# MLP of a two-layer trunk: one fused loop over 256 units, or the whole first product and then the whole second, through memory

## The chip, the cores and the metric

One core of one Trainium2 chip runs the whole kernel. The metric is the device time of one execution in microseconds (us); less is better. The profile is one execution's record of every instruction on the engines: TensorE (PE, with its weight loads as PEld), VectorE (DVE), ScalarE (ACT), GpSimd (POOL) and SyncE (SP), which only issues DMAs.

## The reference

Two layers over x of 1024 tokens x 1024 channels, float32. Each has a mixer (an mLSTM and a windowed attention behind one input projection, then an output projection), and behind it the part that is changed:

```python
h2 = _rmsnorm(x, norm2_g[l])                                   # 1024 x 1024
x = x + jnp.square(jax.nn.relu(h2 @ w_ff1[l])) @ w_ff2[l]      # 1024 x 4096, 4096 x 1024
```

## The kernel before

A float32 product is made of three float32r products: each operand is split into a high part (a cast by ScalarE) and a low part (the operand minus its high part, by GpSimd for weights, by VectorE for activations), and TensorE adds high x high, high x low and low x high in PSUM.

A layer has four stages with a barrier of all engines behind each: input projection, attention and convolution, mLSTM with output projection and residual, and the MLP. Each engine's order of work is written out by hand; semaphores that only count up order the engines against each other. Nothing is planned by a program.

The MLP goes over `CH = 16` chunks of 256 hidden units. For a chunk, `hidden_part` makes W1's product in the plain way: 2 x 128 units, 2 halves of 512 tokens, 8 blocks of 128 channels, 3 parts, so 96 matmuls of 512 columns into PSUM banks 6 and 7. ScalarE takes relu and square (`hidden`). The second product, `product`, is by Winograd's form of Strassen's scheme: the 256 units and 1024 columns of W2 and the 512 tokens of a half are cut into 2 x 2 blocks, and 7 block products stand in for 8. It wants sums of blocks: `u_sums` of the activations and `w2_sums` of W2, on VectorE. `u_his`, `w2_hi` and `w1_hi` on ScalarE cast, `u_los` on VectorE and `w1_lo`, `w2_lo` on GpSimd subtract. A chunk has 2 x 7 products of 6 matmuls, 84, and VectorE's `add` adds each of the 14 from two PSUM banks to x in SBUF (`xs`). Some products are accumulated in PSUM on one that has been added once already, so `product` waits for an earlier `add`.

TensorE's order (`halves`) puts 6 to 10 matmuls of the next chunk's first product behind each of the 14 block products, so a chunk of the loop is 84 + 96 = 180 matmuls, and 12 matmuls lie between one block product and the next. The first chunk's hidden product (`hidden_quarter`, 192 matmuls of 256 columns) lies in the norm at the MLP's start; the last chunk has no next one to be mixed with. VectorE's order is 14 adds with `u_sums`, `u_los` and `w2_sums` between them. SP loads W1 and W2 of a chunk (512 KB a DMA) when GpSimd is through with the one before.

## Time and profile before

| | us |
|---|---|
| median of 3 runs (lowest, highest) | 2406.27 (2405.28, 2407.17) |
| profiled execution, whole | 2407.71 |
| its span, first to last instruction | 2405.9 |
| TensorE busy | 2279.0 |
| VectorE busy | 1536.9 |
| ScalarE busy | 801.7 |
| GpSimd busy | 827.4 |
| mean granted TensorE clock, as a share of full speed | 0.969 |

"Busy" counts every instruction from start to end; matmuls overlap, so the step from one start to the next is what a matmul costs. Layer 0's MLP lies at 501 to 1206 us of the span, layer 1's at 1700 to 2406. In a profile's line, L1592 is the line of the code, then come engine, operation, output <- inputs, shape and count.

### The profile page before, as it was taken

To read this page: it belongs to the slowest core of one execution; us is meant where nothing else is said; L and a number is where in the kernel's file an instruction comes from. 1 tells how busy PE (TensorE), PEld (TensorE's weight loads), DVE (VectorE), ACT (ScalarE), POOL (GpSimd) and SP (SyncE) were. 2 spreads that over 40 slices of the span, in tenths; PEclk is the share of its full clock that TensorE was granted. 3 is DMA by queue.
4 is the path that set the end of the run, shared out by engine and by line. 5 is a ranking of instruction groups with operands and counts; after the bars stand their busy time and mean duration, and the time that the engine had idled before them with its cause. 6 is when DMAs were issued, how large, how long until landed. Compare 5 with 4: busy or idle time off the path is not lost.

```text
span 2405.9 us, 36025 instructions
## 1 busy us (share of the span) xinstructions
PE 2279.0 (95%) x12356; PEld 1923.3 (80%) x12356; DVE 1536.9 (64%) x1838; ACT 801.7 (33%) x1436; POOL 827.4 (34%) x641
## 2 busy tenths in 40 slices
PE   6999979988999999999879999799799999999997
PEld 6988868877888888888679888688778888888886
DVE  4048753356777778777740487533567777777876
ACT  4133332233333333333241334322333333333331
POOL 4235421233242424334142453221333424242431
PEclk9999989989999999999989999899899999999999
DMA  6222332202011121211142222322011211112111
GB/s 252 94 70 72 104 110 66 96 18 70 35 52 52 35 70 35 70 35 52 45 150 84 66 86 90 109 66 96 26 63 35 70 35 54 51 35 70 35 52 70
DMA packets 83368, 166.87 MB, mean 69 GB/s; under 512 B 18008, under 2 KB 45272, under 8 KB 83168
## 3 DMA queue, kind: packets, MB, share of 16 engines
q1 hardware_dynamic: 68064, 142.79, 18.0%
q10 hardware_dynamic: 15232, 23.16, 2.7%
q8 instruction: 40, 0.66, 0.1%
q14 instruction: 32, 0.26, 0.0%
HBM read 138.57 MB, written 31.54 MB: 71 GB/s over the span
## 4 chain that ended last, share of the span: by engine, by line
PE 84%; DVE 6%; issue 6%; ACT 2%; POOL 1%; ACTq 1%; DVEq 0%; SPq 0%; POOLq 0%
PE ps L958 29%; PE ps L1229 24%; PE ps L1212 23%; DVE xs L1592 2%; DVE ul L1617 2%; PE ps L1054 1%; PE ps L1130 1%; PE ps L1124 1%; PE ps L1153 1%; PE ps L949 1%; PE ps L1154 1%; DVE y L1278 1%; PE ps L1082 1%; PE ps L1069 1%; PE ps L1126 1%
## 5 line engine op out<-in xcount | busy, mean ns | idle before, releaser
L1592 DVE TENSOR_TENSOR xs<-ps,xs 128x1024 f32<-128x1024 f32 x448 | 546.9, 1221 | 310.1 <-PE ps L1229 307.5
L1229 PE MATMUL ps<-w2h,uh 128*128 128x512 f32 x896 | 356.0, 397 | 35.2 <-DVE xs L1592 19.4
L1212 PE MATMUL ps<-hTh,w1h 128*128 128x512 f32 x960 | 374.2, 390 | 0.0
L1212 PE MATMUL ps<-hTl,w1h 128*128 128x512 f32 x960 | 374.1, 390 | 0.0
L1212 PE MATMUL ps<-hTh,w1l 128*128 128x512 f32 x960 | 374.1, 390 | 0.0
L912 POOL TENSOR_TENSOR w2l<-raw,w2h 128x512 fp32r<-128x512 f32 x128 | 169.1, 1332 | 586.8 <-ACT w2h L700 586.8
L1229 PE MATMUL ps<-w2l,uh 128*128 128x512 f32 x896 | 351.2, 392 | 0.0
L1229 PE MATMUL ps<-w2h,ul 128*128 128x512 f32 x896 | 350.8, 392 | 0.0
L1229 PEld LDWEIGHTS ps<-w2h,uh 128*128 128x128 f32 x896 | 169.3, 189 | 86.6 <-DVE xs L1592 36.3
L912 POOL TENSOR_TENSOR w2l<-tS,w2h 128x512 fp32r<-128x512 f32 x96 | 172.8, 1802 | 183.3 <-ACT w2h L700 183.3
L1212 PEld LDWEIGHTS ps<-hTl,w1h 128*128 128x128 f32 x960 | 180.7, 188 | 38.0
L1212 PEld LDWEIGHTS ps<-hTh,w1h 128*128 128x128 f32 x960 | 180.8, 188 | 37.7
L1212 PEld LDWEIGHTS ps<-hTh,w1l 128*128 128x128 f32 x960 | 180.5, 188 | 37.8
L1229 PEld LDWEIGHTS ps<-w2h,ul 128*128 128x128 f32 x896 | 169.5, 189 | 36.1
L1229 PEld LDWEIGHTS ps<-w2l,uh 128*128 128x128 f32 x896 | 169.7, 189 | 33.8
L908 POOL TENSOR_TENSOR w1l<-rawf,w1h 128x1024 fp32r<-128x1024 f32 x64 | 155.8, 2437 | 99.4 <-ACT w1h L691 95.9
L958 PE MATMUL ps<-whi,hTh 128*128 128x258 f32 x640 | 184.3, 288 | 1.9 <-POOL wlo L834 0.9
L707 ACT ACTIVATE uq<-ps 128x512 f32<-128x512 f32 x120 | 71.8, 599 | 338.4 <-PE ps L1212 335.0
L958 PE MATMUL ps<-wlo,hTh 128*128 128x258 f32 x640 | 181.9, 284 | 0.0
L958 PE MATMUL ps<-whi,hTl 128*128 128x258 f32 x640 | 181.5, 284 | 0.0
L722 ACT CAST uh<-uq 128x1024 fp32r<-128x1024 f32 x64 | 67.3, 1052 | 291.1 <-DVE uS L1609 291.1
L958 PE MATMUL ps<-hTh,whi 128*128 128x512 f32 x384 | 156.0, 406 | 0.0
(198 smaller groups left out, 4295.9 us busy)
## 6 DMA issues: line engine op xcount, KB each, us to landing
raw<-in_wstream SPq DMA_DIRECT2D x104, 512.0 KB, 4.5
rawf<-in_wstream SPq DMA_DIRECT2D x64, 512.0 KB, 4.6
raw<-in_wtoken SPq DMA_DIRECT2D x20, 516.0 KB, 6.1
zD<-zst ACTq DMA_DIRECT2D x80, 129.0 KB, 1.8
xt<-out_y SPq DMA_DIRECT2D x16, 512.0 KB, 3.4
out_y<-xs SPq DMA_DIRECT2D x16, 512.0 KB, 4.0
zq<-zD SPq DMA_DIRECT2D x16, 320.0 KB, 2.7
xs<-in_x ACTq DMA_DIRECT2D x8, 512.0 KB, 11.1
```

The costliest lines, as they stand in the source:

```text
L707: nc.scalar.activation(uq[b][:, a, :], ps[:, bank, :], ACT.Relu).then_inc(f_rel, 1)
L722: nc.scalar.copy(uh[b][:, 0:4, :], uq[b][:].rearrange("p a (h c) -> p (a h) c", c=256)).then_inc(u_hi, 1)
L908: nc.gpsimd.tensor_tensor(w1l[:, a, :], raw1[a][:], w1h[:, a, :].bitcast(F32), ALU.subtract).then_inc(m1_lo, 1)
L912: nc.gpsimd.tensor_tensor(w2l[:, r, :], w2_from(r), w2h[:, r, :].bitcast(F32), ALU.subtract).then_inc(m2_lo, 1)
L949: mm = pe.transpose(ps[:, bank + k // 4, (k % 4) * P:(k % 4) * P + P], ybuf[t % 2][:, k * P:(k + 1) * P], ident[:])
L958: mm = pe.matmul(out_ap, a, b, start=(c == 0), stop=(c == n - 1))
L1054: pe.matmul(ps[0:64, SB + h // 4, m * P:(m + 1) * P], qS[b0:b0 + DH, m * P:m * P + 64], kw0[b0:b0 + DH, :], start=True, stop=True)
L1069: mm = pe.transpose(ps[:, TB + h // 4, (h % 4) * P:(h % 4) * P + P], pr[:, h, :], ident[:])
L1212: mm = pe.matmul(ps[:, 6 + a, :], w, x, start=(c % 24 == 0), stop=(c % 24 == 23))
L1229: mm = pe.matmul(ps[:, BANK[r] + tp, :], u, w[:, r, :], start=(r < 3 and j == 0), stop=(j == 2), skip_group_check=True)
L1592: V.tensor_tensor(y, ps[:, BANK[r]:BANK[r] + 2, :], y, ALU.add).then_inc(f_acc, 1)
L1617: V.tensor_tensor(ul[b][:, 4:7, :], uS[:], uh[b][:, 4:7, :].bitcast(F32), ALU.subtract).then_inc(u_lo, 1)
```

## The change

The MLP is cut in two phases.

**Phase 1** makes the whole of W1's product. Chunks 0 and 1 (`STD = 2`) are made in the plain way (192 matmuls of 256 columns, 96 of 512). Chunks 2 to 15, called steps here, (`pair_1`) are by seven block products too: 128 units x 512 channels x 512 tokens each, 12 matmuls, 84 a step. For this three block sums of the normed activations are made once a layer (`t_step`, ten VectorE ops of 2048 elements; `sum_hi` on ScalarE, `sum_lo` on GpSimd) and `w1_sums` for each step (4 VectorE ops of 512). The seven products are put together into four blocks by ScalarE's `first_copy` and five VectorE adds of a PSUM bank and an SBUF row (`f_w`). Then come relu and square, `u_sums`, `u_his` and `u_los` as before, each now over all 1024 tokens, and `store_u` on SP writes high and low parts of the seven blocks to a DRAM tensor `uD`: eight DMAs a step, 1 KB runs. SBUF for this is won by spilling x (`xs`) to `out` and reading it back.

**Phase 2** makes the second product over `GR = 8` groups of 512 units. `product_2` has 12 matmuls (two units of 256 accumulate in PSUM), 168 a group; `load_u` reads a group's u, 8 DMAs. `add` is needed once for 12 matmuls instead of once for 6. `w2_sums`, `w2_hi` and `w2_lo` work on 1024 elements at once instead of 512, once a group.

Semaphores of small ops in other stages are merged, and `hTh`, `hTl` become one tensor `hT` in another order, with the same instructions.

The pieces of the diff below belong, in their order, to SP (`store_u` to `stream_2`), ScalarE (the first `phase_1`), GpSimd (`sum_lo`, `w1_lo`), TensorE (`pair_1`, `product_2`) and VectorE (the second `phase_1` and all behind it).

```diff
-        hTh = wide("hTh", [P, KT, S], F32R)
-        hTl = wide("hTl", [P, KT, S], F32R)
+        hT = wide("hT", [P, 2, 2, KT, 512], F32R)
...
+        uD = nc.dram_tensor("uD", [CH, 2, P, 7, 2, 256], F32, kind="Internal").ap()
...
+        ORD1, ORDZ = (1, 6, 5, 2, 7, 3, 4), (2, 1, 6, 5, 7, 3, 4)
+        ORD2 = (1, 5, 6, 3, 7, 2, 4)
+        PARTS = ((4, 7), (0, 4))
...
+                def store_u(j, c):
+
+                    for part in range(2):
+                        i0, i1 = PARTS[part]
+                        sp.wait_ge(u_hi, l * (2 * CH) + (j * 4 + (2 * c + part + 1)))
+                        alone(sp)
+                        for b in range(2):
+                            sp.dma_start(uD[j * 2 + c, b, :, i0:i1, 0, :], uh[:, i0:i1, b * 256:b * 256 + 256].bitcast(F32)).then_inc(u_hst, 16)
...
+                def stream_1(j, c):
+
+                    sp.wait_ge(m1_lo, l * FM + (j * 14 + (7 * (c - STD) + 4 * STD + 7)))
+                    alone(sp)
+                    if c == 0:
+                        load_w1(j, 1, raw1)
+                        store_u(j - 1, 1)
+                    else:
+                        load_w1(j + 1, 0, raw1)
+                        store_u(j, 0)
...
+                def stream_2(g, first):
+
+                    sp.wait_ge(m2_lo, l * (7 * GR) + (g * 7 + 7))
+                    alone(sp)
+                    load_w2(g + 1)
...
+                    for b in range(2):
+                        load_u(g + 1, b, 0, g * 14 + (7 * b + 4))
+                        load_u(g + 1, b, 1, g * 14 + (7 * b + 7))
...
+                def phase_1(j, c):
...
+                        hidden(jp, cp, 3, A12, None, f_w, added(l, jp, cp, 5))
+                    w1_hi(j, c, 6)
+                    first_copy(j, c, made(l, j, c, 1))
+                    u_his(jp, cp)
+                    w1_hi(jn, cn, 0); w1_hi(jn, cn, 1); w1_hi(jn, cn, 2)
+                    hidden(j, c, 0, A11, ps[:, 4 * s, :], f_m, made(l, j, c, 2))
+                    w1_hi(jn, cn, 3)
+                    hidden(j, c, 1, A22, None, f_w, added(l, j, c, 3))
+                    w1_hi(jn, cn, 4)
+                    hidden(j, c, 2, A21, None, f_w, added(l, j, c, 4))
+                    w1_hi(jn, cn, 5)
...
+                sum_lo(0, 1); sum_lo(1, 2)
+                w1_lo(1, 0, 0); w1_lo(1, 0, 1); w1_lo(1, 0, 2)
+                sum_lo(2, 4)
+                sum_lo(3, 3)
+                for pos in range(3, 7):
+                    w1_lo(1, 0, pos)
...
+                def pair_1(j, c):
+
+                    o = 4 * (c % 2)
+                    pe.wait_ge(f_rel, l * (4 * CH) + (j * 8 + 4 * (c - 1)))
+                    for pos, (r, bank, first) in enumerate(((1, 0, True), (6, 1, True), (5, 2, True), (2, 0, False), (7, 3, True), (3, 2, False), (4, 3, False))):
+                        pe.wait_ge(m1_lo, made(l, j, c, r))
+                        if r in (2, 3, 4):
+                            pe.wait_ge(f_w, added(l, j, c, {2: 1, 3: 2, 4: 3}[r]))
...
+                        product_1(r, o + bank, first, True)
...
+                def product_2(g, b, r, first):
...
+                    if r in (6, 7, 3, 4):
+                        pe.wait_ge(y_acc, n + POS2[{6: 1, 7: 6, 3: 5, 4: 7}[r]] + 1)
...
+                def phase_1(j, c):
...
+                        V.tensor_tensor(up, ps[:, (4 - o) + 3, :], up, ALU.add).then_inc(f_w, 1)
+                    u_sums(jp, cp)
+                    dve.wait_ge(f_m, made(l, j, c, 6))
+                    dve.wait_ge(f_m1, l * (CH - STD) + (j * 2 + (c - 1)))
+                    V.tensor_tensor(u[:, A12, :], ps[:, o + 1, :], u[:, A12, :], ALU.add).then_inc(f_w, 1)
+                    u_los(jp, cp, 0)
+                    dve.wait_ge(f_m, made(l, j, c, 5))
+                    dve.wait_ge(f_w, added(l, j, c, 1))
+                    V.tensor_tensor(u[:, A22, :], ps[:, o + 2, :], u[:, A12, :], ALU.add).then_inc(f_w, 1)
+                    w1_sums(jn, cn)
+                    u_los(jp, cp, 1)
+                    dve.wait_ge(f_m, made(l, j, c, 7))
+                    dve.wait_ge(f_w, added(l, j, c, 2))
+                    V.tensor_tensor(u[:, A22, :], ps[:, o + 3, :], u[:, A22, :], ALU.add).then_inc(f_w, 1)
+                    dve.wait_ge(f_m, made(l, j, c, 3))
+                    V.tensor_tensor(u[:, A21, :], ps[:, o + 2, :], u[:, A12, :], ALU.add).then_inc(f_w, 1)
...
+                u_los(LAST, 0, 1)
+                dve.wait_ge(f_m, FZ + POSZ[7] + 1)
+                dve.wait_ge(f_w, AZ + 3)
+                V.tensor_tensor(u[:, A22, :], ps[:, 7, :], u[:, A22, :], ALU.add).then_inc(f_w, 1)
...
+                w2_sums(0, 1)
+                u_sums(LAST, 1)
+                add(0, 0, 1, True)
+                u_los(LAST, 1, 0)
+                add(0, 0, 5, True)
+                u_los(LAST, 1, 1)
...
+                def half_1(g, first, more):
+                    add(g, 1, 1, first)
                     if more:
-                        w2_sums(p + 1, 0)
-                    add(p, 1, 0)
+                        w2_sums(g + 1, 0)
+                    add(g, 1, 5, first)
+                    if more:
+                        w2_sums(g + 1, 1)
+                    for r in (6, 3, 7, 2, 4):
+                        add(g, 1, r, first)
```

## Rows read from the trace of the kernel before

**Rows 1.** The page, part 1: busy time, share and instructions of each engine.
```profile
PE 2279.0 (95%) x12356; PEld 1923.3 (80%) x12356; DVE 1536.9 (64%) x1838; ACT 801.7 (33%) x1436; POOL 827.4 (34%) x641
```

**Rows 2.** Stretches of layer 0's MLP: length, busy us of each engine, clock, DMA.
```profile
549.00:1172.50 623.50, 618.15 (x2700) 506.95 (x2700) 476.96 (x450) 215.15 (x312) 228.18 (x135) 1.00 0.14 47
1172.50:1200.00 27.50, 22.57 (x85) 16.23 (x84) 19.42 (x20) 3.01 (x4) 0.44 (x1) 0.94 0.20 77
```

**Rows 3.** Chain of waits inside the loop: start us, us, what.
```profile
788.45 1.36 PE ps L1212 x6
...
792.35 1.63 DVE ul L1617
```

**Rows 4.** Timeline of VectorE and GpSimd in the loop: start us, us, what.
```profile
761.07 2.53 DVE L1603 TENSOR_TENSOR uS<-uq 128x256 f32<-128x256 f32 x1
...
771.95 0.95 DVE L1617 TENSOR_TENSOR ul<-uS,uh 128x768 fp32r<-128x768 f32 x1
...
792.35 3.01 DVE L1617 TENSOR_TENSOR ul<-uS,uh 128x768 fp32r<-128x768 f32 x1
795.28 1.21 DVE L1592 TENSOR_TENSOR xs<-ps,xs 128x1024 f32<-128x1024 f32 x1
...
802.55 2.53 DVE L1603 TENSOR_TENSOR uS<-uq 128x256 f32<-128x256 f32 x1
...
792.13 2.40 POOL L908 TENSOR_TENSOR w1l<-rawf,w1h 128x1024 fp32r<-128x1024 f32 x1
794.50 2.00 POOL L912 TENSOR_TENSOR w2l<-tS,w2h 128x512 fp32r<-128x512 f32 x1
...
798.98 1.29 POOL L912 TENSOR_TENSOR w2l<-tS,w2h 128x512 fp32r<-128x512 f32 x1
```

**Rows 5.** The same two engines behind the norm of layer 0's MLP.
```profile
533.29 1.23 DVE L1284 TENSOR_TENSOR hTl<-ps,hTh 128x1024 fp32r<-128x1024 f32 x1 [2.24 <-ACT hTh L483]
...
537.95 1.51 DVE L1603 TENSOR_TENSOR uS<-uq 128x256 f32<-128x256 f32 x1
...
539.14 2.88 POOL L912 TENSOR_TENSOR w2l<-raw,w2h 128x512 fp32r<-128x512 f32 x2
```

**Rows 6.** Groups by line: busy us, mean ns of one, idle before.
```profile
L1592 DVE TENSOR_TENSOR xs<-ps,xs 128x1024 f32<-128x1024 f32 x448 | 546.9, 1221 | 310.1 <-PE ps L1229 307.5
...
L1614 DVE TENSOR_TENSOR ul<-uq,uh 128x1024 fp32r<-128x1024 f32 x64 | 77.8, 1216 | 2.2 <-ACT uh L722 2.2
...
L707 ACT ACTIVATE uq<-ps 128x512 f32<-128x512 f32 x120 | 71.8, 599 | 338.4 <-PE ps L1212 335.0
L722 ACT CAST uh<-uq 128x1024 fp32r<-128x1024 f32 x64 | 67.3, 1052 | 291.1 <-DVE uS L1609 291.1
```

**Rows 7.** DMA queues by packets, and a W2 load's issues and landing.
```profile
q1 hardware_dynamic: 68064, 142.79, 18.0%
q10 hardware_dynamic: 15232, 23.16, 2.7%
...
800.53 0.92 SPq L418 DMA_DIRECT2D raw<-in_wstream  x2
...
DMA to landing us min/median/max: 3.2/4.0/8.4
```

**Rows 8.** Timeline of TensorE around its waits in layer 0's MLP.
```profile
540.56 0.28 PE L958 MATMUL ps<-hTh,w1l 128*128 128x256 f32 x1
548.71 0.79 PE L1229 MATMUL ps<-w2h,uh 128*128 128x512 f32 x1 [7.87 <-ACT uq L714]
...
1184.52 0.74 PE L1229 MATMUL ps<-w2h,uh 128*128 128x512 f32 x1 [2.38 <-DVE xs L1592]
...
1188.04 0.40 PE L1229 MATMUL ps<-w2h,ul 128*128 128x512 f32 x1
...
1199.04 0.40 PE L1229 MATMUL ps<-w2h,ul 128*128 128x512 f32 x1
```

More of the change, by code:

```diff
@@ L392, in load_c @@
                     sp.dma_start(xt[p][:], out_t[i]).then_inc(c_xt[p], 16)
+                    if not (first or (isinstance(j, int) and i < 2)):
+                        sp.dma_start(out_t[i - 2], xs[:, i - 2, :]).then_inc(s_spill, 16)
                 def unit_c(k):
@@ new lines, in _, with load_w2, load_u @@
+                stream_1(1, 0); stream_1(1, 1)
+                with sp.Fori(2, LAST) as j:
+                    stream_1(j, 0); stream_1(j, 1)
+                stream_1(LAST, 0)
+                def load_w2(g):
+                    for k in range(2):
+                        for a in range(2):
+                            sp.dma_start(raw2[:, k, a, :], wstream[l, g * 8 + (UB + UC + 4 * k + 2 + a)]).then_inc(m2_raw, 16)
+                def load_u(g, b, part, upto):
+                    i0, i1 = ((0, 4), (4, 7))[part]
+                    if upto is not None:
+                        sp.wait_ge(y_m, l * YM + upto)
+                        alone(sp)
+                    for k in range(2):
+                        sp.dma_start(uk[b][k][:, i0:i1].bitcast(F32), uD[g * 2 + k, b, :, i0:i1]).then_inc(u_ld[b][part], 16)
@@ new lines, in _ @@
+                sp.wait_ge(f_m, l * FM + FM - 7 + POSZ[6] + 1)
+                alone(sp)
+                for t in (0, 1):
+                    sp.dma_start(xs[:, t, :], out_t[t]).then_inc(s_x[t], 16)
+                sp.wait_ge(f_m, l * FM + FM - 7 + POSZ[5] + 1)
+                alone(sp)
+                for t in (4, 5):
+                    sp.dma_start(xs[:, t, :], out_t[t]).then_inc(s_x[t], 16)
+                store_u(LAST, 0)
+                sp.wait_ge(f_m, l * FM + FM)
+                alone(sp)
@@ L931, in _ @@
+                with pool.Fori(2, LAST + 1) as j:
+                    for c in range(2):
+                        for pos in range(7):
+                            w1_lo(j, c, pos)
+                with pool.Fori(0, GR) as g:
+                    for r in ORD2:
+                        w2_lo(g, r)
                 barrier(pool, p_pool, (p_pe, p_sp, p_dve, p_act), l * PHASES + 4)
@@ new lines, in product_1 @@
+                def product_1(r, bank, first, last):
+                    xh, xl = right(r)
+                    s = SLOT[r]
+                    for k in range(4):
+                        h_, l_ = w1s[:, s, 0, k * P:k * P + P], w1s[:, s, 1, k * P:k * P + P]
+                        for i, (w, x) in enumerate(((h_, xh), (h_, xl), (l_, xh))):
+                            mm = pe.matmul(ps[:, bank, :], w, x[:, k, :], start=(first and k == 0 and i == 0), stop=(k == 3 and i == 2),
+                                           skip_group_check=True)
+                    mm.then_inc(f_m, 1)
@@ L1248, in _ @@
+                for b in range(2):
+                    for r in ORD2:
+                        product_2(0, b, r, True)
+                alone(pe)
+                with pe.Fori(1, GR) as g:
+                    for b in range(2):
+                        for r in ORD2:
+                            product_2(g, b, r, False)
                 barrier(pe, p_pe, (p_act, p_sp, p_dve, p_pool), l * PHASES + 4)
@@ new lines, in raw_of, with t_step @@
+                def raw_of(t):
+                    return tf[t][:, 1]
+                def t_step(n, out_, a, b, op):
+                    if n in (2, 3, 4, 5, 6, 9):
+                        dve.wait_ge(t_sum, l * 10 + n)
+                    V.tensor_tensor(out_, a, b, op).then_inc(t_sum, 1)
+                H = {k: v.bitcast(F32) for k, v in b_at_h.items()}
+                L = {k: v.bitcast(F32) for k, v in b_at_l.items()}
+                Z = [hTf[:, 1, i, 0:4, :] for i in range(2)]
+                SUB = ALU.subtract
@@ new lines, in _, with w2_sums @@
+                phase_1(1, 0); phase_1(1, 1)
+                with dve.Fori(2, LAST) as j:
+                    phase_1(j, 0); phase_1(j, 1)
+                phase_1(LAST, 0)
+                def w2_sums(g, part):
+                    n = l * (4 * GR) + g * 4
+                    b11, b12, b21, b22 = [raw2[:, :, a, c:c + 512] for a in range(2) for c in (0, 512)]
+                    if part == 0:
+                        dve.wait_ge(m2_raw, l * (64 * GR) + (g * 64 + 64))
+                        V.tensor_tensor(tS[0][:], b12, b11, ALU.subtract).then_inc(m2_sum, 1)
```

733 lines of the change are left out of this document (434 added, 299 removed).

## The prediction

> **What bounds the kernel now.** I read the page first: TensorE is busy 95% of the span, VectorE 64%, GpSimd 34% [rows 1]. The reader is to see from this that only work on TensorE, or something that makes TensorE wait, can move the time. The table of stretches of layer 0 then shows where TensorE isn't fed [rows 2]: the MLP's loop, 549.0 to 1172.5, holds 2700 matmuls in 623.5 us, and the last chunk's 84 matmuls take 27 us. One matmul of 512 columns starts 1.36 / 6 = 0.227 us after the one before [rows 3]. So 180 of them, one chunk of the loop, need 40.8 us; the first op of its `u_sums` comes back after 802.55 - 761.07 = 41.5 us [rows 4]. The 0.7 us between is the key to this change, and the chain of waits shows where it comes from [rows 3]: a subtraction on VectorE (`u_los`) ends the row of matmuls. The subtraction of 768 elements at 792.35 took 3.01 us, while another instance of the same line took 0.95 [rows 4]. GpSimd held its own subtraction from 792.13 to 794.53, and VectorE finished 0.83 us after that; the GpSimd op behind it took 2.00 instead of 1.29 us [rows 4]. At 539 both engines had work waiting, and they took turns: three 256-element ops of VectorE took 1.5 us each, the first at 537.95, while GpSimd's of 512 took 1.44 [rows 5]. The adds that read PSUM were never held up: the mean of 448 is 1221 ns, and one ran its usual 1.21 us at 795.28 inside a GpSimd op [rows 4, 6]. I call this **the turn**: a VectorE op with both inputs in SBUF and a GpSimd op do not overlap; the one that comes first runs to its end.
>
> **Prices.** VectorE with two SBUF inputs: 1.22 us at 1024 elements and 0.95 at 768, so by the slope 0.68 at 512 (0.6 from start to start), 1.75 at 1536 and 2.3 at 2048. GpSimd: 1.29 at 512, 2.4 at 1024, so 4.6 at 2048. ScalarE: 1.05 at 1024, 0.60 at 512, so 1.5 and 1.9 at the larger two. Add of 512 from PSUM: 0.68, as in SBUF, since the 1024 cost the same [rows 4, 6]. Two loads of 512 KB: 0.5 between the issues and 4.0 to land, so 4.5 us [rows 7].
>
> **What is removed.** Per layer the first product falls from 1536 matmuls of 512 columns (counting 192 of 256 columns as 96) to 192 in two plain chunks and 14 x 84 = 1176 in the others. That is 168 fewer, 38.1 us a layer, 76 us in all. The second product keeps its 1344. The Trainium skill's TensorE: Matmul & The Clock Gate, Back-to-back issue gap, gives N / 2.4 + 2.5 ns, 216 ns, where this trace has 227; by the page the gain would be 72.5 us. Layer 0 needs 658.9 us now, from the last small matmul's start at 540.56 to the last one's end at 1199.44 [rows 8]. After the change TensorE's own work there is (96 + 1176 + 1344) x 0.2267 = 593.1 us. The waits decide the rest.
>
> **First phase, one step of 84 matmuls, 19.05 us.** Seven products of 2.72 us. VectorE does five adds from PSUM (3.3 us), `u_sums` and `w1_sums` (8 x 0.6), `u_los` (1.75 + 2.3); GpSimd does seven `w1_lo` (9.0). The turn is thus held 8.9 + 9.0 = 17.9 of 19.05 us, and in a fixed order. I walk one step from its first matmul, with GpSimd three subtractions behind, as it turns out to be: four `w1_lo` alternate with the four `u_sums`, the last `w1_lo` ends at 5.4 and `u_sums` at 6.7; add for product 2, 7.4; `u_los` of 1536 can start at 7.7, when ScalarE's `u_his` has ended, and ends 9.4; add, 10.1. SP issues the next W1 at 5.5, and it lands at 10.0. `w1_sums` with one `w1_lo` between takes 3.8, to 13.9; `u_los` of 2048, 16.2; add, 16.9. Only then may product 4 start, due at 16.3. It ends at 19.7 to 20.0, with GpSimd again behind by three. Turned round once more it settles near **20.1 us, 1.05 over**. Bounds: 0 if turns fall well, 2.5 if one more GpSimd op gets in front of `u_los`. Twelve such steps: 12.6 us (0 to 30).
>
> **Start.** `t_step` adds ten VectorE ops of 2048 elements (23 us) and four GpSimd ops of 2048 (18.4), while the first `w1_lo` wait behind them in GpSimd's order. From the end of the norm at 534.5 [rows 5] to the add ahead of product 4 in `phase_1(1, 0)` the turn must be held 23 + 18.4 + 8.1 (`u_los` twice) + 4.9 (`u_sums` twice) + 4.9 (`w1_sums` twice) + 10.3 (eight `w1_lo`) = 69.6 us, to 604; the load of W1 for the step behind adds some 5 in which nobody can use it, and the add 0.7, so product 4 starts near 610 to 611. TensorE could be there at 540.6 + 21.8 + 16.3 = 578.7. That is 32 us of waiting in four or five pieces; now it is 7.9 [rows 8]. After a stall of 2.38 us TensorE ran 8 matmuls at 0.427 us each, a half-speed stretch that cost 1.6 us [rows 8]; most of these stretches lie ahead of another wait, I add 2. Together 34 (20 to 45).
>
> **Between the phases.** In the last step `w2_sums` and the first two `w2_lo` (2.4 each) stand on VectorE and the turn ahead of `u_los`, which stands ahead of the add that product 4 needs: 22.8 instead of 16.3, 6.5 late. Then `add(0, 0, 1)`, needed by the third product of phase 2, stands behind `w2_sums(0, 1)` and `u_sums(LAST, 1)`, which waits for ScalarE's last squares, and ScalarE waits in order for the third `w2` sum; four `w2_lo` of 2.4 us get turns between the four sums. I get 11 us, and 2 more for the next two adds. With a slow stretch 22 us (6, if no turn falls badly, to 30).
>
> **Second phase, a group of 168 matmuls, 38.1 us.** Half 0 has only adds: no wait. In half 1 (time from its first matmul) the first add ends 4.1, as GpSimd starts `w2_lo` to 6.4. Two 1024-element `w2_sums` end at 8.8, the add of product 5 at 10.0: product 3, due 8.2, waits 1.8. The next `w2_lo` holds 8.9 to 11.3, the other two sums end 13.6, the add of product 6 at 14.9, and product 7, due 12.7, waits 2.2. **4.0 us a group, seven groups: 28 a layer.** Bounds: with no turn lost, 0.3 a group; with the half-speed stretch after each, 6. I add 3 for a few stretches: mine are a little shorter than the 2.38 us that had one. So 31 (2 to 42). The end of the layer, now 27.5 us for 84 matmuls [rows 2], needs no wait any more; that is in the 593.1.
>
> **The stores and loads through memory.** A step stores 3.67 MB in 3584 runs of 1 KB, 224 for each of 16 DMA engines. The ACT queue q10 carried 15232 packets of 1.5 KB on average in 2.7% of 16 engines' span, 68 ns each [rows 7]; at that price, too high for 1 KB, the stores take 15.3 us. W1's 16 packets of 4 KB for each engine take 3.2 at q1's 102 ns for 2.1 KB. That is 18.5 of 20 us. SP needs 0.5 us for each of ten issues. Its `store_u` stands behind the wait for the last `w1_lo`, at 5.5, when the first half of `u_his` is ready only at 7.5, so it is late for nothing; the last store is issued at 16.4, lands some 4 us later, and `first_copy`, which waits for it, is due at 22.9. In phase 2 a group loads 7.3 MB of u and 2 of W2 in 38 us, issued most of a group ahead. So 0, with the bound in the rivals. The spill of x before phase 3 and its return lie beside the norm and the last W1 step. Other edits (merged semaphores, the order inside `hT`) cost nothing: the same instructions on the same queues.
>
> **Sum.** 593.1 + 34 + 12.6 + 22 + 31 = 692.7 against 658.9: 34 us more a layer, 68 in all. Against the profiled execution, 2407.7 with a span of 2405.9, and so 1.4 above the median shown, this gives 2475 us.
>
> **Rivals.** (1) *The turn costs little*: ops queue so that VectorE mostly comes first, waits at the lower bounds: 20 + 0 + 6 + 2 = 28 a layer, so 593.1 + 28 = 621, 38 less: 2330. Halfway, 2400. For it: VectorE has 36% idle, and the loop now loses only 0.7 us to it. Against: at 539 the two alternated strictly. It decides once the waits in a layer sum to less than 66 us. (2) *Memory binds the first phase*: each step becomes its eight stores and two loads. If the stores went one by one, each at half the 4.0 us that a load takes to land [rows 7], a step would need 8 x 2.0 + 4.5 = 20.5 to 22 us, 28 steps x 1.9 = 50 more at the upper end: 2525. Against: loads issued 0.5 us apart land together. The Trainium skill's DMA: Bandwidth & Descriptors, Anatomy of one DMA, gives 2.0 us plus bytes / 436 GB/s for each; eight in a row would be 24 us and two loads 6, an estimate of 2700 for the kernel, if nothing overlapped. (3) *Half speed after every stall*: 1.6 us behind each of 14 groups and half of the steps, 45 more: 2520. (4) *It does what it says and only that*: 76 less and the old edges stay, 2330, the same time as (1) and as unlikely.
>
> **Chances.** Forecast (2420 to 2510) 0.63; (1) with (4) 0.18, of which 0.15 faster and 0.03 within 0.2% (what a measurement of this kernel can tell from none); (2) 0.07; (3) 0.12. Slower 0.82. The range 2398 to 2530 leaves out most of (1) and the worst of (2).
>
> **What would show it.** TensorE's starts of one first-phase step 20 us apart, with a gap ahead of its last product released by VectorE; in phase 2 two gaps of 1.8 and 2.2 us in every second half; `w2_sums` at 2 us and more where alone they'd take 1.2; 30 us of gaps behind 562. I am wrong if `u_los` and the sums run at their bare prices, or if gaps are released by a DMA.

## The result, and the profile after

The changed kernel takes 2469.07 us, the median of 4 runs (2465.62 to 2472.09), beside 2405.99 us (2405.28 to 2407.17, 4 runs) of the kernel before: ratio 1.0261, 95% interval 1.0243 to 1.0279. It is 63 us slower; 68 were forecast. Its profiled execution took 2465.62 us.

The page after, parts 1 and 3: busy time, share and instructions of each engine, and the DMA queues.
```profile
PE 2231.7 (91%) x12020; PEld 1875.0 (76%) x12020; DVE 1470.6 (60%) x1632; ACT 858.2 (35%) x1444; POOL 1065.7 (43%) x685
...
q1 hardware_dynamic: 209888, 394.47, 45.9%
```
TensorE has the 336 fewer matmuls that were promised, 12020 instead of 12356 [rows 1], and the span is longer all the same: it is waits that were bought. VectorE has less to do than before, GpSimd more, and q1 moves 394 MB instead of 143 [rows 7].

Timeline of TensorE in layer 0 of the kernel after: start us, length, what, and in brackets the idle time before it and what ended it. The end of a group is modelled, so the time lost at a wait is start minus start, less 0.2267 us for each matmul between.
```profile
537.28 2.98 PE L1183 MATMUL ps<-hT,w1s 128*128 128x256 f32 x17
...
591.14 11.19 PE L1445 MATMUL ps<-hT,w1s 128*128 128x512 f32 x36 [12.93 <-DVE uf L1920]
606.86 4.61 PE L1445 MATMUL ps<-tT,w1s 128*128 128x512 f32 x12 [4.53 <-DVE uf L1929]
...
843.60 3.03 PE L1445 MATMUL ps<-tT,w1s 128*128 128x512 f32 x12 [1.31 <-DVE uf L1929]
867.53 5.49 PE L1445 MATMUL ps<-tT,w1s 128*128 128x512 f32 x12 [4.24 <-DVE uf L1982]
888.52 24.60 PE L1493 MATMUL ps<-w2s,uk 128*128 128x512 f32 x96 [9.74 <-DVE xs L1961]
921.33 4.59 PE L1493 MATMUL ps<-w2s,uk 128*128 128x512 f32 x12 [8.21 <-DVE xs L1961]
927.95 37.27 PE L1493 MATMUL ps<-w2s,uk 128*128 128x512 f32 x156 [2.03 <-DVE xs L1961]
966.71 3.01 PE L1493 MATMUL ps<-w2s,uk 128*128 128x512 f32 x12 [1.49 <-DVE xs L1961]
971.27 35.66 PE L1493 MATMUL ps<-w2s,uk 128*128 128x512 f32 x156 [1.55 <-DVE xs L1961]
1008.41 3.02 PE L1493 MATMUL ps<-w2s,uk 128*128 128x512 f32 x12 [1.49 <-DVE xs L1961]
...
1225.07 1.29 PE L1493 MATMUL ps<-w2s,uk 128*128 128x512 f32 x5
```
The last small matmul starts near 539.2 and the last one of the layer near 1226.1: 687 us, where 692.7 were forecast and 658.9 were needed before [rows 8]. TensorE's own work was taken at 593.1, so 94 us are lost, and the rows say where. The last product of the first pair starts at 606.86 and could have at 539.2 + 168 x 0.2267 = 577.3: 29.6. From there twelve steps take 843.60 - 606.86 = 236.7, or 19.73 each, 0.68 over the 19.05 of their matmuls: 8.2. The last step gives 23.93, 4.9 late, and the 36 matmuls from 867.53 to 888.52 take 20.99 instead of 8.16, 12.8 late. In group 0 the 96 matmuls from 888.52 and the 12 from 921.33 lose 11.0 and 3.9. Then each of six groups has two waits: 971.27 - 966.71 - 2.72 = 1.84 and 1008.41 - 971.27 - 35.37 = 1.77, 3.61 a group and 21.7 in six; 1.6 more is a slow stretch behind 927.95.

VectorE in the second phase of the kernel after, groups by line and shape, 941 to 1199 us: busy us, mean ns.
```profile
L1944 DVE TENSOR_TENSOR raw<-raw 128x1024 f32<-128x1024 f32 x6 | 20.5, 3424 | 0.0
L1947 DVE TENSOR_TENSOR tS<-raw,tS 128x1024 f32<-128x1024 f32 x6 | 13.5, 2251 | 0.0
```
Four subtractions of one size: the first and the last (L1943 and L1949, not shown, 1216 and 1226 ns) run at their bare 1.22 us, and two take 3.42 and 2.25. These are the two waits of a group, nearly as the walk had them: the second sum stands behind the first `w2_lo` (the walk had the first sum behind it too), the third behind the rest of the second.

VectorE and SyncE in the first group of the second phase: the wait that nobody had forecast.
```profile
917.78 1.23 DVE L1943 TENSOR_TENSOR tS<-raw 128x1024 f32<-128x1024 f32 x1 [8.83 <-DMA raw<-in_wstream]
...
888.39 9.62 SPq L476 DMA_DIRECT2D uD<-uh  x4
...
904.81 4.28 SPq L508 DMA_DIRECT2D raw<-in_wstream  x4
```
VectorE waits for the W2 of group 1, which SyncE issues only at 904.8, behind the eight stores of the last chunk's u, the first of them at 888.4. It is used 13.0 us after its issue, where a load of W2 before took 4.0 to land [rows 7]. The last `w2_lo` of group 0, for which the load waits, had ended at 889.6.

Stretches of the kernel after: the steps of the first phase, the turn between the phases, the second phase.
```profile
606.86:843.60 236.74, 233.69 (x1009) 189.44 (x1009) 189.82 (x181) 150.00 (x217) 145.81 (x85) 0.99 0.70 240
843.60:927.95 84.35, 60.13 (x228) 47.50 (x228) 54.61 (x38) 28.07 (x33) 37.82 (x16) 0.86 0.89 332
927.95:1226.30 298.35, 280.12 (x1212) 227.66 (x1212) 169.84 (x125) 46.80 (x45) 122.84 (x47) 0.99 0.57 209
```
The last two numbers are the busy share of the 16 DMA engines and GB/s. It was 0.14 in the loop before [rows 2]; now it is 0.70 in the first phase and 0.89 between the phases.

### The profile page after: what moved, and what is told of

Read it like the earlier page. It is cut to its first block, busy times and chain, and to the rows that moved or that the text cites. A ratio compares the mean times of both kernels' runs of the same rounds, so it can differ in the third digit from the quotient of the medians.

```text
span 2463.8 us, 36690 instructions
## 1 busy us (share of the span) xinstructions
PE 2231.7 (91%) x12020; PEld 1875.0 (76%) x12020; DVE 1470.6 (60%) x1632; ACT 858.2 (35%) x1444; POOL 1065.7 (43%) x685
## 4 chain that ended last, share of the span: by engine, by line
PE 57%; issue 20%; POOL 9%; DVE 6%; SPq 4%; DMA 2%; ACT 1%; ACTq 0%; POOLq 0%; DVEq 0%
PE ps L1183 28%; PE ps L1493 19%; POOL w1s L1124 8%; SPq L476 2%; DVE xs L1961 2%; DVE tS L1947 1%; PE ps L1445 1%; POOL tT L1131 1%; PE ps L1278 1%; SPq L482 1%; PE ps L1174 1%; PE ps L1354 1%; PE ps L1348 1%; DMA raw<-in_wstream 1%; PE ps L1377 1%
## 5 line engine op out<-in xcount | busy, mean ns | idle before, releaser
L1493 PE MATMUL ps<-w2s,uk 128*128 128x512 f32 x2688 | 628.5, 395 | 76.9 <-DVE xs L1961 76.9
L1493 PEld LDWEIGHTS ps<-w2s,uk 128*128 128x128 f32 x2688 | 509.6, 191 | 195.7 <-DVE xs L1961 89.8
L1961 DVE TENSOR_TENSOR xs<-ps,xs 128x1024 f32<-128x1024 f32 x224 | 273.9, 1223 | 268.8 <-PE ps L1493 267.3
L1445 PE MATMUL ps<-hT,w1s 128*128 128x512 f32 x1344 | 322.9, 397 | 37.2 <-DVE uf L1920 25.9
L1445 PEld LDWEIGHTS ps<-hT,w1s 128*128 128x128 f32 x1344 | 258.2, 193 | 93.8 <-DVE uf L1920 26.7
L1445 PE MATMUL ps<-tT,w1s 128*128 128x512 f32 x1008 | 251.6, 404 | 29.2 <-DVE uf L1929 17.8
L1445 PEld LDWEIGHTS ps<-tT,w1s 128*128 128x128 f32 x1008 | 193.3, 194 | 82.9 <-DVE uf L1929 30.0
L1183 PE MATMUL ps<-hT,whi 128*128 128x512 f32 x768 | 245.7, 401 | 0.0
L1183 PE MATMUL ps<-whi,hT 128*128 128x258 f32 x1280 | 239.0, 286 | 2.0 <-DVE hT L1539 1.4
L1183 PEld LDWEIGHTS ps<-whi,hT 128*128 128x128 f32 x1280 | 201.6, 191 | 4.0 <-issue 3.5
```

The costliest lines, as they stand in the source:

```text
L1183: mm = pe.matmul(out_ap, a, b, start=(c == 0), stop=(c == n - 1))
L1445: mm = pe.matmul(ps[:, bank, :], w, x[:, k, :], start=(first and k == 0 and i == 0), stop=(k == 3 and i == 2), skip_group_check=True)
L1493: mm = pe.matmul(ps[:, bank + tp, :], u, w2s[r][:, w, k, :], start=(r in (1, 2, 5) and k == 0 and i == 0), stop=(k == 1 and i == 2), skip_ ...
L1961: V.tensor_tensor(y, ps[:, bank:bank + 2, :], y, ALU.add).then_inc(y_acc, 1)
```

## The experiments

My theory was the turn: a VectorE op with two inputs in SBUF and a GpSimd op exclude each other, and with that the order of the queues sets the waits. The rivals were the plain length of VectorE's queue, and memory. Unless it is said otherwise, a kernel is the changed one with one edit. The kernel before ran beside each on its chip, at 2405.2 to 2405.8 us. One thing must be kept in mind: the twelve steps of the first phase are not equally long from trace to trace. In layer 0 they take 236.7 us in the changed kernel's trace and 239.8 to 244.6 in those of the next three edits and of the order between the phases, none of which touches that phase. Differences of a few us between two kernels can come from there.

**The sums of W2 in half 0.**
```
 with dve.Fori(1, GR - 1) as g:
     for r in ORD2:
         add(g, 0, r, False)
+        if r in (3, 7, 2, 4): w2_sum(g + 1, {3: 0, 7: 1, 2: 2, 4: 3}[r])
-    half_1(g, False, True)
+    half_1(g, False, False)
```


> Groups 1 to 6 of the second phase make the next group's four w2_sums one by one behind the last four adds of half 0, where GpSimd has nothing to do, instead of in half 1. My theory (the turn): a sum takes its bare 1.22 us there and fits the 1.5 us that VectorE has between two adds, each w2_lo takes its bare 2.4 us, and the two waits of TensorE in every half 1 (1.84 and 1.77 us, 3.61 a group) go: 12 x 3.61 = 43 us less, 2426 us. Rival one (memory): the next W2 has not landed by then, VectorE waits for it with the adds of half 0 behind, and TensorE waits in half 0 instead: 2460 to 2480 us. Rival two (the waits come from the PSUM banks or the loads of u, not from the sums): no change, 2469.


Measured 2426.30 us (2421.38 to 2430.54, 4 runs), 42.8 less than 2469.07, ratio to before 1.0089 (1.0066 to 1.0111). TensorE then runs the rest of the layer in one piece. Timeline of TensorE, and groups of VectorE and GpSimd from 945 to 1199 us:
```profile
931.00 275.32 PE L1493 MATMUL ps<-w2s,uk 128*128 128x512 f32 x1212 [1.49 <-DVE xs L1973]
...
L1961 DVE TENSOR_TENSOR raw<-raw 128x1024 f32<-128x1024 f32 x6 | 7.3, 1214 | 0.0
L1135 POOL TENSOR_TENSOR w2s<-raw,w2s 128x1024 fp32r<-128x1024 f32 x24 | 57.6, 2399 | 122.2 <-ACT w2s L944 122.2
```
The op that took 3424 ns takes 1214 where GpSimd is idle. All 1212 matmuls follow one another. The time is the forecast to the microsecond, with some luck: in layer 0 the stretch of six groups lost its waits and its slow stretch, 23 us where the forecast counted 21.7, while the twelve steps took 4.9 us longer in this trace.

**GpSimd's op in the second phase cut short.** It leaves out 448 of 512 columns of `w2_lo`, where ScalarE puts a copy of W2's tile; the sums stay in half 1.
```
 w2_hi: + nc.scalar.copy(w2s[r][:, 1, :, 64:512], w2_from(r)[:, :, 64:512])
 w2_lo: nc.gpsimd.tensor_tensor(w2s[r][:, 1, :, 0:64], w2_from(r)[:, :, 0:64], ..., ALU.subtract)
```


> In the second phase GpSimd's w2_lo subtracts 64 of each 512 columns only (128 elements, some 0.5 us instead of 2.4); ScalarE copies the other 448 columns of W2's tile there, which is not the remainder that the computation wants. The sums stay where the changed kernel has them, in half 1. It tells the turn from the plain length of VectorE's queue. The turn: two sums of 1.22, the first late by one short op, end before the add of product 5 is due to matter; the waits of 1.84 and 1.77 us in half 1 fall under 0.3 each, the sums run at 1.2 to 1.7 us, and between the phases 13 us of held time go too: 2405 to 2425 us. Rival (the sums delay the adds by their own length): both waits stay within 0.3 us of what they are, 2465 us.


One run, 2433.27 us. Timeline of TensorE, and one of each op from VectorE's and GpSimd's:
```profile
925.62 43.77 PE L1494 MATMUL ps<-w2s,uk 128*128 128x512 f32 x180 [14.29 <-DVE xs L1962]
969.95 38.37 PE L1494 MATMUL ps<-w2s,uk 128*128 128x512 f32 x168 [0.56 <-DVE xs L1962]
1008.89 1.43 PE L1494 MATMUL ps<-w2s,uk 128*128 128x512 f32 x5 [0.57 <-DVE xs L1962]
```
```profile
963.54 1.48 DVE L1945 TENSOR_TENSOR raw<-raw 128x1024 f32<-128x1024 f32 x1
...
963.24 0.70 POOL L1136 TENSOR_TENSOR w2s<-raw,w2s 128x128 fp32r<-128x128 f32 x1 [21.30 <-ACT w2s L945]
```
A group now takes 1008.89 - 969.95 = 38.94 us, 0.86 over its matmuls instead of 3.61, with the four sums in the same places. So at least three quarters of the wait came from GpSimd's op. The rest isn't all queue: the second and third sum, 1.48 and 1.42 us, are still 0.26 and 0.2 late beside the short op. The total missed its 2405 to 2425: the wait for group 1's W2 grew to 14.3 us, since TensorE reached it sooner and the load, counted from the end of the twelve steps, came only 1 us sooner; those steps took 5.2 us longer in this trace.

**Group 1's W2 issued ahead of the last stores.**
```
-store_u(LAST, 1)
 def stream_2(g, first):
     sp.wait_ge(m2_lo, l * (7 * GR) + (g * 7 + 7))
     load_w2(g + 1)
     if first:
+        store_u(LAST, 1)
```


> Only SyncE's order between the phases is changed: the load of group 1's W2 is issued ahead of the stores of the last chunk's u instead of behind them. In the changed kernel that load is issued at 904.8, when the stores at 888.4 to 904.5 are out, and VectorE waits 8.8 us for it, which TensorE sees as 8.2 and 2.0 us of waiting in group 0 and a slow stretch behind. My theory: the load goes out as soon as the last w2_lo of group 0 is done (889.6) and lands before half 1; group 0 then has the two waits of 1.8 us that the other groups have. 10.2 + 0.6 - 3.6 = 7 us and 1.6 of slow clock, 9 us a layer, 18 in all: 2451 us. Rival (the load waits for the bandwidth that the stores and u's loads take, not for its place in the queue): it lands late all the same, 2465 to 2470.


Measured 2453.54 us (2445.88 to 2458.57), 15.5 less, for 18 forecast. Timeline of TensorE:
```profile
898.02 24.68 PE L1493 MATMUL ps<-w2s,uk 128*128 128x512 f32 x96 [9.65 <-DVE xs L1961]
924.18 3.04 PE L1493 MATMUL ps<-w2s,uk 128*128 128x512 f32 x12 [1.48 <-DVE xs L1961]
928.74 35.68 PE L1493 MATMUL ps<-w2s,uk 128*128 128x512 f32 x156 [1.53 <-DVE xs L1961]
```
Group 0 has the two waits of every other group. The long one came from the load's place in SyncE's order.

**The four large subtractions of the start on VectorE.**
```
 def sum_lo(n, t): ...
-    nc.gpsimd.tensor_tensor(lo_, raw_, hi.bitcast(F32), ALU.subtract)
+    V.tensor_tensor(lo_, raw_, hi.bitcast(F32), ALU.subtract)
```
with its four calls moved from GpSimd's order into VectorE's, behind u_sums(0, 0), t_step 5, w1_sums(1, 0) and u_sums(0, 1).

> At the start of the first phase the four subtractions of 2048 elements that GpSimd makes (sum_lo) are put on VectorE, where one takes 2.3 us instead of 4.5; nothing else. My theory (the turn: what counts is the sum of what both engines hold): 4 x (4.5 - 2.3) = 9 us less of held time ahead of product 4 of the first pair, which starts near 598 instead of 606.9; 9 us a layer, and with a slow stretch less 18 to 22 in all: 2449 us. Rival one (VectorE's own queue is the bound, GpSimd's work is beside it): 9.2 us more on VectorE, 2 x 9 more, 2487. Rival two (the start waits for the load of W1 in the first step, 6.5 us in the trace, whatever comes before): no change, 2469.


Measured 2445.23 us (2443.37 to 2447.28), 23.8 less, ratio 1.0162 (1.0145 to 1.0179). To give VectorE, the busier of the two, nine microseconds more work a layer made the kernel faster, as it should if GpSimd's eighteen are gone from the same turn; that VectorE's queue alone is the bound, which forecast 2487, is refuted. Timeline of TensorE:
```profile
599.49 2.88 PE L1435 MATMUL ps<-tT,w1s 128*128 128x512 f32 x12
```
Product 4 starts at 599.5 instead of 606.9; 598 was forecast. That is 7.4 us, and in layer 1, counted from the same matmuls, it is 9.6: 17 of the 23.8. The rest lies in the steps behind and isn't explained by the edit: in layer 0 of this trace W1 was used 4.9 to 7.0 us after its issue, and product 4 of the twelfth step starts at 843.42, not sooner than in the changed kernel.

**The order between the phases.**
```
-w2_sums(0, 0)
 u_los(LAST, 0, 1)
 ... add of product 7 ...
+w2_sums(0, 0)
 ...
-u_sums(LAST, 1); add(0, 0, 1); u_los(LAST, 1, 0); add(0, 0, 5); u_los(LAST, 1, 1); adds 6, 3, 7, 2, 4
+adds 1, 5, 6; u_sums(LAST, 1); add(0, 0, 3); u_los(LAST, 1, 0); adds 7, 2; u_los(LAST, 1, 1); add(0, 0, 4)
```


> VectorE's order between the phases: w2_sums(0, 0) behind u_los(LAST, 0, 1) and the add of product 7, on which product 4 waits; and the first three adds of phase 2 ahead of u_sums(LAST, 1), whose results only the stores of the last chunk's u need, with u_sums and u_los in the gaps of half 0. Nothing is left out. My theory: TensorE's waits of 4.2 and 9.7 us there come from this order and the turn. The first falls under 1 us; the second to about 2 us (the third sum stands behind add 4, then comes w2_lo of product 6). 4 + 7 = 11 us less a layer, with a slow stretch less 12 to 14; against it the last stores and so group 1's W2, which stands behind them, come 4 to 8 us later and lengthen the wait of 8.2 us by as much. Net 2 x 6 = 12 less: 2457 us, and the wait in half 1 of group 0 over 10 us. Rival (the held time itself is the bound, order does not matter): within 3 us of 2469.


Measured 2469.50 us (2466.64 to 2473.87): nothing, where 12 less were forecast. The wait of 4.2 us went, that of 9.7 fell to three of 1.8, 3.7 and 1.1, 8 us in all for 11 forecast, and all of it came back in one place, the wait for group 1's W2, 18.3 instead of 8.2. Timeline of TensorE:
```profile
877.29 11.22 PE L1493 MATMUL ps<-w2s,uk 128*128 128x512 f32 x48 [1.76 <-DVE xs L1961]
892.24 9.79 PE L1493 MATMUL ps<-w2s,uk 128*128 128x512 f32 x36 [3.73 <-DVE xs L1961]
...
924.46 5.20 PE L1493 MATMUL ps<-w2s,uk 128*128 128x512 f32 x12 [18.29 <-DVE xs L1961]
```
I had written this down as the price against, 4 to 8 us of 12; it was all that was won.

**Each store of u made twice** (the second to a memory of its own).


> Each store of u is made twice, the second to a memory of its own that nobody reads; SyncE issues 18 DMAs a step instead of 10, and ScalarE's waits for the stores count both. In the changed kernel the DMA engines are busy 0.69 of a step of 19.4 us, 13.4 us, of which W1's load takes some 3.2. If that price holds, a step has 23.6 us of work for them: with 14 steps a layer at 4 to 5 us more, 115 to 140 us in all, 2585 to 2610 us, the DMAs having had a third of room. If the stores were hidden with much room (my prediction's term of nothing, at its 15.3 us a step for the stores), the same side. Rival (each DMA's fixed time, not its bytes, is what would bind, and eight were not far from it): 28 steps of 34 us or more, 2850 us. Rival two (the stores lie beside everything): 2469.


One run, 2664.51 us, above the 2585 to 2610 forecast and far below 2850. Stretch of nine steps of layer 0:
```profile
648.74:884.35 235.61, 194.48 (x756) 156.11 (x756) 135.75 (x135) 111.14 (x163) 106.47 (x63) 0.89 0.97 320
```
A step takes 235.61 / 9 = 26.2 us with the DMA engines busy 0.97 of it: 25.4 us of work for them, where the changed kernel has 0.70 x 19.73 = 13.8. The 3.67 MB of stores cost 11.6 us, not the 15.3 of my sum and not the 10.2 of this expectation. The time of the DMA engines binds here, and the rival with a fixed time for each DMA, 34 us or more a step, is out; whether it is bytes or the number of packets that costs, this run doesn't tell. My size was low: a step is 6.5 us longer, not 4 to 5, and the stretch between the phases grew as well: in group 0 TensorE waited 29.8 us for group 1's W2, where it had waited 8.2.

**All four edits together.**


> The four edits together: w2_sums in half 0, the W2 load of group 1 ahead of the last stores, sum_lo on VectorE, the new order between the phases. If they add up as timed alone against 2469 (43, 15.5, 24 and 0 less) the time is 2386 us, 0.8% under the kernel before. My theory says more than that: the new order alone brought TensorE 7 us ahead, all of which went into a longer wait for group 1's W2; with that load no longer behind the stores it should count, 5 to 7 us a layer: 2374 us. Rival (memory binds between the phases, where the DMA engines are busy 0.92 of the time): the loads of u, x and W2 only land later, 2386 to 2395 us, with TensorE's waits in group 0 released by DMAs or by adds that wait for x.


Measured 2394.23 us (2389.93 to 2397.04), ratio to before 0.9956 (0.9942 to 0.9969). It is the first version under the kernel before, but the 2374 of my theory fell; the rival's 2386 to 2395 stands. SyncE and VectorE between the phases:
```profile
877.96 2.97 SPq L508 DMA_DIRECT2D raw<-in_wstream  x4
...
897.96 1.23 DVE L1945 TENSOR_TENSOR tS<-raw 128x1024 f32<-128x1024 f32 x1 [9.11 <-DMA raw<-in_wstream]
```
W2 is now issued 27 us earlier and lands 17 to 20 us after its issue: the DMA engines are busy 0.96 from 840 to 870 and 0.89 from 870 to 925 us.

**The last stores later still**, on the kernel with the four edits.
```
 stream_2(0, True)
+store_u(LAST, 1)
-with sp.Fori(1, GR - 1) as g:
+with sp.Fori(1, GR - 2) as g:
     stream_2(g, False)
+stream_2(GR - 2, False, True)     # waits for the last chunk's stores
```


> The kernel with the four edits, and the stores of the last chunk's u moved once more, behind all loads of group 1 (only group 7 reads that chunk; its loads wait for the stores). In the kernel with four edits group 1's W2 is issued at 878.0 and lands 17 to 20 us later, with the stores issued right behind it and x and u loading before it; the DMA engines are 0.89 to 0.96 busy there. My theory now (memory binds between the phases, as bytes in flight together): without those 3.67 MB, 10 us at 366 GB/s, W2 lands near 888, TensorE's wait of 9.6 us in half 1 of group 0 falls to 1 or 2, and the 3.6 us in group 1, released by the W2 of group 2 that lands late, goes too: 10 us a layer, 2374 us. Rival (each transfer in its place of the queue, the stores behind take nothing from it): within 3 us of 2394.


Measured 2404.17 us (2396.76 to 2412.21, 12 runs), 10 us slower than with the four edits, where 20 faster were forecast. TensorE and SyncE:
```profile
944.80 252.61 PE L1484 MATMUL ps<-w2s,uk 128*128 128x512 f32 x1104 [8.66 <-DVE xs L1976]
```
```profile
920.90 2.99 SPq L476 DMA_DIRECT2D uD<-uh  x4
...
931.14 4.49 SPq L508 DMA_DIRECT2D raw<-in_wstream  x4
```
Group 1's W2 came hardly sooner: TensorE's wait for it is 8.2 us, not 9.6, so the stores behind it were not what mainly held it. What loads ahead of it (half of group 0's u and four tiles of x, 5.8 MB) is left as the likely cause. And the stores now stand ahead of group 2's W2, which made the wait in group 1 8.7 us instead of 3.6, some 5 us a layer. The first phase took 4.8 us longer in layer 0 of this trace than in that of the four edits, which the edit does not explain.

**Three more changes of order**, on the kernel just shown: u_sums(LAST, 1) one add later, the w2_sums of group 0 behind the adds of products 5 and 6, and at the start ScalarE's last plain square ahead of `sum_hi(3, 3)`.


> As the run above, and three changes of order: u_sums(LAST, 1) one add later; in half 1 of group 0 the two w2_sums behind the adds of products 5 and 6 instead of 1 and 5; at the start ScalarE's last plain square ahead of the third t copy, so that u_sums(0, 1) on VectorE, now idle for 4.2 us ahead of it, can start. Under the turn and the queues as read from the traces: 4 us a layer at the start (part of a wait of 12.8 us), 1 to 3 us a layer between the phases: 10 to 14 us under the run above, near 2362 us. Rival (the start is bound by the load of W1 behind it, or by held time alone, wherever the idle lies): no difference to the run above.


Measured 2403.49 us (2397.99 to 2411.85, 11 runs): no difference to the run above, so the rival stands. TensorE's start:
```profile
580.26 10.56 PE L1436 MATMUL ps<-hT,w1s 128*128 128x512 f32 x36 [6.36 <-POOL w1s L1125]
597.64 4.95 PE L1436 MATMUL ps<-tT,w1s 128*128 128x512 f32 x12 [6.81 <-DVE uf L1932]
```
The wait ahead of product 2 fell by half and came back ahead of product 4. How much of that is held time and how much is the load of W1 behind it, this run does not tell.

**W1's load alone on the queues**, on the kernel with the four edits, which ran again beside it as the measure.
```
 load_w1(j + 1, 0, raw1)
+sp.wait_ge(m1_raw[0], l * (16 * CH) + (j * 32 + 64))
 store_u(j, 0)
```
and the same in the other branch.

> The kernel with the four edits once more, as the measure for the next two on the same chip. Its first phase depends on when W1 lands: VectorE waited 7.8 us for it between 640 and 850 us of that kernel's trace and 12.5 us in that of the run with the later stores, though both have the same program there. If that is memory and not the program, this time falls between 2394 and 2404 us and its trace shows between 8 and 13 us of such waits.

> The four edits, and in the first phase SyncE waits until W1 has landed before it issues the stores of u that now follow 2 us behind the load. My theory: those stores are what lengthens the load's landing from 4.5 to 5 or 6 us; alone it lands in 4.5, VectorE's waits for W1 (8 to 17 us in 210 us of the traces) fall under 3, and the first-phase steps come down to 19.1 to 19.3 us: 0.4 to 0.8 us in 26 steps, 10 to 20 us less than the kernel with four edits, and less spread. Against it: the stores go 4 us later; the last of them is bound by u_los, which comes after the landing anyway, so first_copy should not see it. Rival (the landing time is the memory's own, or the later stores delay first_copy): no gain, or up to 10 us more.


Measured 2391.16 us (2388.30 to 2396.77) for the measure, under the 2394 to 2404 expected of it, with 11.4 us of waits for W1 where 8 to 13 were expected; and 2379.08 us (2377.46 to 2379.84) with the wait: 12.1 less, ratio to before 0.9891 (0.9876 to 0.9906). VectorE's groups from 640 to 850 us, the measure first, then the kernel with the wait:
```profile
L1858 DVE TENSOR_TENSOR sS<-rawf 128x512 f32<-128x512 f32 x10 | 6.9, 692 | 11.4 <-DMA rawf<-in_wstream 11.4
```
```profile
L1862 DVE TENSOR_TENSOR sS<-rawf 128x512 f32<-128x512 f32 x10 | 6.9, 693 | 4.8 <-DMA rawf<-in_wstream 4.7
```
SyncE's issues in the kernel with the wait:
```profile
700.01 0.99 SPq L460 DMA_DIRECT2D rawf<-in_wstream  x2
705.08 2.81 SPq L476 DMA_DIRECT2D uD<-uh  x4
```
The first eleven steps take 19.0 to 19.2 us here, and TensorE shows no wait at all in them; in the twelfth it waits 1.0. W1 is used 4.5 to 4.8 us after its issue. VectorE still waits 4.8 us, not under 3 as forecast, but early enough to cost nothing up to the last step. Layer 1 is less even: four of its twelve steps take 19.3 to 20.1 us. The spread of the runs fell from 8.5 to 2.4 us, over four runs.

**Group 1's W2 ahead of u and x as well**, on that kernel: `load_w2(1)` moved ahead of `load_u(0, 1, ...)`.


> As the run above, and between the phases group 1's W2 is issued as soon as the last w2_lo of group 0 is done, ahead of the second half of u for group 0 and four tiles of x instead of behind them. My theory (memory is the bound there, and only the order of arrival can be chosen): W2 lands 6 us earlier, TensorE's wait of 9.6 us in half 1 of group 0 falls to 2 or 3, and the u and x that come later cost 3 to 5 us there: 2 to 5 us a layer under the run above, 4 to 10 in all. Rival (all three are needed at once, so that the order moves the wait and does not shorten it): within 2 us of the run above.


Measured 2378.65 us (2371.57 to 2379.41, 4 runs), 0.4 under the run above: the rival stands. TensorE:
```profile
875.77 4.59 PE L1491 MATMUL ps<-w2s,uk 128*128 128x512 f32 x12 [3.56 <-DVE xs L1983]
883.52 11.20 PE L1491 MATMUL ps<-w2s,uk 128*128 128x512 f32 x36 [3.16 <-DMA uk<-uD]
```
The one wait of 9.4 us is gone; in its place there are several, the two shown and four of 1.3 to 4.2 us behind them, and some of them are now for u itself. The traces are less clear than the time: from the first matmul of phase 2 to the end of the last wait in group 1 they have 78.2 and 78.9 us in the two layers where the kernel of the run above has 80.8 and 80.2, a gain of 4 us at the forecast's lower end, and steps of up to 19.95 us in the first phase take half of it back in layer 0. That the sum of the bytes counts between the phases fits with this, but no run moved fewer of them.

## Why the prediction was right, and where it was not

The time, 2469 for 2475, and the reason for most of it held. For each term of the sum in layer 0, in us:

| term | forecast | measured | held? |
|---|---|---|---|
| start | 34 | 29.6 | yes; sum_lo on VectorE moved it by 7.4 of 9 |
| twelve steps of phase 1 | 12.6 | 8.2 | in part: the last lap of the walk too dear, W1's landing too cheap |
| between the phases | 22 | 17.7 | yes; both waits fell when w2_lo was cut short |
| phase 2, six groups | 24 | 21.7 | yes, shown twice |
| phase 2, group 0 | 4 | 14.9 | no: the wait for group 1's W2 is missing |
| slow stretches of phase 2 | 3 | 1.6 | near |
| sum | 99.6 | 93.7 | |

That the sum came out so near is partly luck. Five terms were too high, by 17 us together, and one, group 0, was too low by 11: the prediction took the stores and loads at 0 there, and the run that moved W2's load ahead of the stores shows that wait as theirs.

**The turn** is shown: the same op takes 3424 ns beside GpSimd's and 1214 away from it, and the waits fall both when VectorE's ops are moved and when GpSimd's are made short. This agrees with the Trainium skill, SBUF — State Buffer, Who interferes with whom: a VectorE op with two SBUF inputs contends with a GpSimd op that reads SBUF. That the one that comes first holds the ports for the whole instruction is stated there for VectorE's two-port modes; here the trace shows it for subtractions with two inputs. Rival (1), that the turn costs little, needed under 66 us of waits a layer; there were 94.

**Phase 1: the walk was right up to product 4, and wrong in where it settles.** GpSimd is three subtractions behind at the step's first matmul, as the prediction has it, and the last of them runs to 4.8 us of the step. VectorE, GpSimd, SyncE and TensorE in the step after that starts at 709.07:
```profile
710.94 1.79 DVE L1849 TENSOR_TENSOR uf<-uf 128x512 f32<-128x512 f32 x1
...
712.14 1.73 POOL L1124 TENSOR_TENSOR w1s<-rawf,w1s 128x512 fp32r<-128x512 f32 x1
...
714.19 0.99 SPq L460 DMA_DIRECT2D rawf<-in_wstream  x2
...
716.15 1.76 DVE L1862 TENSOR_TENSOR uf<-uf,uh 128x1536 fp32r<-128x1536 f32 x1 [0.34 <-ACT uh L881]
...
719.09 0.69 DVE L1868 TENSOR_TENSOR sS<-rawf 128x512 f32<-128x512 f32 x1 [0.58 <-DMA rawf<-in_wstream]
...
720.30 1.78 DVE L1871 TENSOR_TENSOR sS<-sS,rawf 128x512 f32<-128x512 f32 x1
...
725.67 3.03 PE L1445 MATMUL ps<-tT,w1s 128*128 128x512 f32 x12
```
Counted from 709.07, W1 is issued at 5.1 (the walk has 5.5), the first `u_los` starts at 7.1 (7.7), W1 is used at 10.0 (10.0), and product 4 starts at 16.6 (16.9). Two of the `u_sums` and one of the `w1_sums` took turns with `w1_lo`, 1.7 to 1.8 us where 0.69 is bare. `u_los` ran bare in all twelve steps, 1.76 and 2.28 us; the walk has it so too, so the sign "I am wrong if `u_los` and the sums run at their bare prices" could not tell anything by `u_los`. The step of the prediction that failed is "Turned round once more it settles near 20.1 us": ten of the twelve steps take 19.4 to 19.8.

What sets a step's length can be read from the traces. In the changed kernel, in all steps but the first and the last, the step from one product 4 to the next is 14.54 to 14.58 us longer than the time from W1's issue to its use, which is 4.8 to 5.2 (the last step, 20.64, has 6.2 and 14.5). The chain closes on itself: the turn holds back the last `w1_lo`, behind it SyncE issues W1, then come `w1_sums`, with one more turn, `u_los`, the add and product 4. With W1 used after 4.5 us, the prediction's price, such a step would take 14.55 + 4.5 = 19.05, an estimate, and just what its matmuls need. So the turn fills the step and W1's late landing makes it overflow; of the 8.2 us lost, 6.1 are that landing over 4.5 and 2.0 the first step, with its slow stretch behind the long wait. **"The stores and loads: 0"** is the term that should have held the 6.1. With W1 alone on the queues it is used after 4.5 to 4.8 us in layer 0 and eleven of the twelve steps there take 19.0 to 19.2, with 12 us off the time. Why it takes 5 us in some steps and 6 in others of the same kernel stays open: with W1 alone, too, the kernel with W2 ahead has some steps of 19.4 to 19.95.

**Memory.** Rival (2) as I priced it, one store after the other, is refuted; the 50 us did not come. But a weak form of it was true at three places: W1's landing, W2 of group 1 (its place in SyncE's order, 15.5 us over both layers), and the stretch between the phases, where 0.89 of the DMA time is taken. The transfers do overlap: from 700 to 800 us a step's eight stores and two loads take 3.4 to 5.1 us each from issue to landing (medians), 42 us in sum, and a step takes 19.5. The Trainium skill's DMA: Bandwidth & Descriptors, Anatomy of one DMA, from whose fixed 2.0 us the prediction took its 2700, states that figure for a DMA on GpSimd's path. These are SyncE's, and no run here shows the figure; what the runs show is that the transfers are not laid end to end, since the 2700 is 230 us too high.

**Half speed after every stall**, rival (3), did not come in phase 2: the 12 matmuls behind each of the waits of 1.84 us take the usual 3.01 us. Those behind the longer ones, 8.21 and 4.24, take 4.59 and 5.49. Between the phases the mean granted clock is 0.86 of full speed, in phase 2 0.99.

**A matmul's price.** The 216 ns that the prediction took from the Trainium skill's TensorE: Matmul & The Clock Gate, Back-to-back issue gap, are that section's figure for a matmul by itself; for a stream of weight loads and matmuls it gives about 131 ns at 512 columns. The traces agree with neither: 227 ns in both kernels. The sum went by the trace.

**Open.** What the start is bound by once the large subtractions are off GpSimd is not known, and how much of the stretch between the phases could be won by moving fewer bytes wasn't tried.

## What to carry to other kernels

Count what two engines hold of a shared resource as one queue, in the order of arrival; then moving work onto the busier engine can be a gain, and so can moving it by ten microseconds to where the other is idle. When a change sends data through memory, walk SyncE's order as well as the engines': a load that stands behind stores comes late by their time, and stores issued right behind a load can make it land later (here 5 to 6 us instead of 4.6). The change itself was worth having once its waits were scheduled away: 2379 us against 2406, 1.1% faster, where as made it was 2.6% slower.
